# Where the first half's rows are turned at three layer ends, where a gate turn stands, and buffers of their own for the memory rows

## The reference

```python
def rms_norm(x, gain):
    y = x * lax.rsqrt(jnp.mean(x * x, axis=-1, keepdims=True) + RMS_EPS)
    return y * gain

for i in range(2):                                   # NSA, then SSD
    hn = rms_norm(h, gains[0])
    m = nsa_mixer(hn, ...) if i == 0 else ssd_mixer(hn, ...)
    h = h + rms_norm(m, gains[1])
    f = conv_ffn(rms_norm(h, gains[2]), ...)         # up, conv, silu * , down
    h = h + rms_norm(f, gains[3])
# second block, one layer
mem_n = rms_norm(mem, mem_norm)
u = rms_norm(h, norm_pre_mix)
y_mix, q_mem = gdn_branch(u @ gdn_w_in, ...)
mem_k, mem_v = jnp.split(mem_n @ w_mem_kv, 2, axis=-1)
y = jnp.concatenate([y_mix, memory_attention(q_mem, mem_k, mem_v)], axis=-1) @ w_out
h = h + rms_norm(y, norm_post_mix)
h = h + rms_norm(swiglu(rms_norm(h, norm_pre_ffn), ...), norm_post_ffn)

# inside the NSA mixer, 48 columns of the projection become the gates
gates = sigmoid(proj[..., kv_end:]).reshape(b, s, g, hpg, 3)
```

## Time and profile before

| | us |
|---|---|
| three runs | 1214.59, 1219.58, 1211.85; median 1214.59 |
| the profiled execution | 1215.68 |
| its span in the profile | 1213.9 |
| PE busy / DVE busy / ACT busy | 1180.3 / 847.2 / 651.3 |
| mean granted clock of PE, share of full | 0.998 |

### The profile page before, as it was taken

The page is one execution under the profiler, slowest core; times in us unless marked ns, Lnnn a source line. Parts: engine busy times, 40 slices in busy tenths (PEclk is TensorE's granted clock), DMA queues, the critical chain, the costliest instruction groups (busy, mean ns, idle before and its releaser), DMA issues.

```text
span 1213.9 us, 23231 instructions
## 1 busy us (share of the span) xinstructions
PE 1180.3 (97%) x9876; PEld 1079.3 (89%) x9876; DVE 847.2 (70%) x1299; ACT 651.3 (54%) x1171; POOL 149.0 (12%) x143
## 2 busy tenths in 40 slices
PE   8999999999999999999999999999999999999998
PEld 8887779999879898977999988899989877999986
DVE  6578867888557888886788875857577776655542
ACT  4557646666445666644666663565434534644431
POOL 1220000000002333100000000103443411000000
PEclk9999999999999999999999999999999999999999
DMA  8842135665634443353655664442232322755540
GB/s 304 266 140 88 62 103 218 209 204 183 238 106 148 177 182 141 113 175 112 243 187 197 208 242 156 176 174 105 94 118 71 111 100 87 279 181 198 182 169 35
DMA packets 31623, 196.68 MB, mean 162 GB/s; under 512 B 4000, under 2 KB 5664, under 8 KB 9376
## 3 DMA queue, kind: packets, MB, share of 16 engines
q1 hardware_dynamic: 27504, 185.17, 43.0%
q10 hardware_dynamic: 4016, 10.03, 2.6%
HBM read 193.09 MB, written 1.05 MB: 160 GB/s over the span
## 4 chain that ended last, share of the span: by engine, by line
PE 86%; DVE 6%; ACT 3%; issue 2%; POOL 1%; DMA 1%; ACTq 0%; DVEq 0%; POOLq 0%; SPq 0%
PE bank L514 24%; PE bank L516 23%; PE bank L515 23%; DVE wlo L502 2%; PE bank L1860 1%; ACT whi L495 1%; PE bank L1097 1%; PE bank L1154 1%; PE bank L1181 1%; DMA raw<-in_wall 1%; DVE xT L704 1%; PE bank L2506 1%; PE bank L688 1%; PE bank L2972 1%; PE bank L2449 1%
## 5 line engine op out<-in xcount | busy, mean ns | idle before, releaser
L502 DVE TENSOR_TENSOR wlo<-raw,whi 128x1024 fp32r<-128x1024 f32 (+1 forms) x325 | 390.0, 1237 | 92.8 <-ACT whi L495 92.1
L514 PE MATMUL bank<-xT,wlo 128*128 128x256 f32 x1544 | 434.4, 281 | 6.2 <-DVE xc L1566 2.1
L516 PE MATMUL bank<-xT,whi 128*128 128x256 f32 x1544 | 428.6, 278 | 0.0
L515 PE MATMUL bank<-xT,whi 128*128 128x256 f32 x1544 | 428.6, 278 | 0.0
L495 ACT ACTIVATE whi<-raw 128x1024 fp32r<-128x1024 f32 (+1 forms) x349 | 349.5, 1048 | 115.8 <-PE bank L516 82.8
L514 PEld LDWEIGHTS bank<-xT,wlo 128*128 128x128 f32 x1544 | 288.6, 187 | 10.6 <-issue 3.9
L515 PEld LDWEIGHTS bank<-xT,whi 128*128 128x128 f32 x1544 | 288.8, 187 | 0.9 <-issue 0.5
L516 PEld LDWEIGHTS bank<-xT,whi 128*128 128x128 f32 x1544 | 288.5, 187 | 0.2
L633 POOL TENSOR_TENSOR rr<-rr,nhalf 128x1 f32<-128x1 f32 x34 | 24.8, 729 | 714.4 <-DVE rr L621 526.7
L514 PE MATMUL bank<-whi,xT 128*128 128x256 f32 (+1 forms) x352 | 104.6, 297 | 6.6 <-DVE xT L704 6.6
L514 PE MATMUL bank<-whi,gT 128*128 128x512 f32 x264 | 104.4, 396 | 0.0
(11 more groups left out here) (369 smaller groups left out, 1654.1 us busy)
## 6 DMA issues: line engine op xcount, KB each, us to landing
raw<-in_wall SPq DMA_DIRECT2D x173, 1024.0 KB, 4.9
grow<-in_rows ACTq DMA_DIRECT2D x13, 512.0 KB, 5.6
h<-in_x SPq DMA_DIRECT2D x4, 256.0 KB, 5.6
dsk<-in_rows ACTq DMA_DIRECT2D x4, 256.0 KB, 3.5
memx<-in_mem ACTq DMA_DIRECT2D x1, 1024.0 KB, 9.9
out<-h SPq DMA_DIRECT2D x4, 256.0 KB, 2.1
masks<-in_masks SPq DMA_DIRECT2D x1, 580.0 KB, 12.6
D<-Tx ACTq DMA_DIRECT2D x4, 128.0 KB, 6.0
```

The lines of the kernel that those rows point to most:

```text
L502: e.tensor_tensor(wlo[i % NHL][:, o:o + w], raw[i % NRAW][:, o:o + w], whi[i % NHL][:, o:o + w], SUB).then_inc(*up("dve.low", p))
L514: e.matmul(out, a[1], b[0], start=start, stop=False)
L515: e.matmul(out, a[0], b[1], start=False, stop=False)
L516: return e.matmul(out, a[0], b[0], start=False, stop=stop)
```

## The change

It has three parts. The reordering on PE at a layer's end stands in `pe_down`, which may call a function between its two halves n=0 and n=1; the callers give `pe_norm_turn(e, k, 0)` for the last chunk of t=1.

```diff
-        def pe_down(e, t, i, src, ks, base, start, stop, k0=0):
+        def pe_down(e, t, i, src, ks, base, start, stop, between=None):
...
                 if stop and t and n == 0:
                     d.then_inc(*up("pe.early", i))
+                if between and n == 0:
+                    between()
...
-        def pe_boundary(e, k, a=None):
-            pe_norm_turn(e, k, 0)
-            if a is not None:
-
-                e.wait_ge(*at("dve.norm", "mp", a, 0, 0))
-                e.wait_ge(*at("act.norm", "add", a, 0, 1))
-                pe_fill_first(e, FFN_AT.index(k), k)
-                pe_busy(e, 0, 6)
+        def pe_boundary(e, k, a):
+
+
+            e.wait_ge(*at("dve.norm", "mp", a, 0, 0))
+            e.wait_ge(*at("act.norm", "add", a, 0, 1))
+            pe_fill_first(e, FFN_AT.index(k), k)
+            pe_busy(e, 0, 6)
             pe_norm_turn(e, k, 1)
...
         def pe_ssd_first(e):
 
-            pe_norm_turn(e, 2, 0)
...
-                pe_down(e, t, C_GO + c, ygT, ks, 2 * t, c == 0, c == 5)
+                pe_down(e, t, C_GO + c, ygT, ks, 2 * t, c == 0, c == 5,
+                        (lambda: pe_norm_turn(e, 6, 0)) if (t, c) == (1, 5) else None)
...
-            pe_ffn(e, 0, 1)
+            pe_ffn(e, 0, 1, None, lambda: pe_norm_turn(e, 2, 0))
...
-                pe_down(e, t, C_SO + c, ysT, (2 * c, 2 * c + 1), 2 * t, False, c == 7)
+                pe_down(e, t, C_SO + c, ysT, (2 * c, 2 * c + 1), 2 * t, False, c == 7,
+                        (lambda: pe_norm_turn(e, 3, 0)) if (t, c) == (1, 7) else None)
```

```diff
+        ffd = ExitStack()
+        sb([128, 2, 22, 256], st=ffd, name="below")
+        mT = [sb([128, 8, 256], f32r, ffd, "mT") for _ in range(2)]
+        ffd.close()
...
+        def rows_of(k):
+            return mT if k == 4 else xT
...
             for i in range(2):
-                run(pe_tm(e, C_M + 2 + i, 6 + i, 256))
+                run(pe_tm(e, C_M + 2 + i, 6 + i, 256, None, mT))
...
+            split.to(C_M + 3)
+            for t in range(2):
+                act_norm_high(e, 5, t)
             split.to(C_M + 3 + AHEAD)
-            e.wait_ge(*at("pe.proj", C_M + 3))
-            for n in range(2):
-                for t in range(2):
-                    act_norm_high(e, 5, t, (n,))
...
+            for t in range(2):
+                dve_norm_low(e, 5, t)
             for i in range(2):
                 split.to(C_M + 2 + i + AHEAD)
                 e.wait_ge(*at("pe.proj", C_M + 2 + i))
...
-            for n in range(2):
-                for t in range(2):
-                    dve_norm_low(e, 5, t, (n,))
```

```diff
-                q = pe_fm(e, QC[c4], QB[c4])
-                next(q)
+                run(pe_fm(e, QC[c4], QB[c4]))
                 if c4 == 0:
                     e.wait_ge(*at("act.nsa", "sigmoid"))
                     pe_few_turn(e, aP[0], 4, 48).then_inc(*up("pe.nsa", "gates"))
-                run(q)
...
                 split.to(5 + c4 + AHEAD)
+                act_q(e, c4)
                 if c4 == 0:
                     e.wait_ge(*at("pe.nsa", "gates"))
```

More of the change, by code:

```diff
@@ L386, in build @@
         pr = [sb([128, 512], st=ffm, name="pr") for _ in range(2)]
+        sb([128, 1024], st=ffm, name="rest")
         memx = sb([128, 2, 1024], st=ffm, name="memx")
         ffm.close()
+        ffd = ExitStack()
+        sb([128, 2, 22, 256], st=ffd, name="below")
+        mT = [sb([128, 8, 256], f32r, ffd, "mT") for _ in range(2)]
+        ffd.close()
         sst = ExitStack()
@@ L414, in build @@
         y1 = xs[:, 512:1024]
+        gk = ExitStack()
+        kmT = sb([128, 4, 256], st=gk, name="kmT")
+        vm = sb([128, 2, 512], st=gk, name="vm")
+        gk.close()
         gd = ExitStack()
@@ L429, in build @@
         ma = ExitStack()
-        kmT = sb([128, 4, 256], st=ma, name="kmT")
-        vm = sb([128, 2, 512], st=ma, name="vm")
         qmT = sb([128, 4, 256], st=ma, name="qmT")
@@ L519, in pe_ready, with pe_fm @@
             e.wait_ge(*at(low_on(i), ENDS[i] - 1))
-        def pe_fm(e, i, bank, layer=None):
+        def pe_fm(e, i, bank, layer=None, rows=xT):
             pe_ready(e, i)
@@ L530, in pe_fm @@
                     t = pe_three(e, banks[bank][:, 256 * m:256 * m + 256], [v[:, k, 128 * m:128 * m + 128] for v in w],
-                                 [x[:, k, :] for x in xT], k == 0, k == 7)
+                                 [x[:, k, :] for x in rows], k == 0, k == 7)
                 if m == 0:
@@ L534, in pe_fm, with pe_tm @@
             t.then_inc(*up("pe.proj", i))
-        def pe_tm(e, i, bank, n, layer=None):
+        def pe_tm(e, i, bank, n, layer=None, rows=xT):
             pe_ready(e, i)
@@ L543, in pe_tm @@
                 for k in range(8):
-                    t = pe_three(e, banks[bank][:, 256 * s:256 * s + n], [x[:, k, 128 * s:128 * s + 128] for x in xT],
+                    t = pe_three(e, banks[bank][:, 256 * s:256 * s + n], [x[:, k, 128 * s:128 * s + 128] for x in rows],
                                  [v[:, k, :] for v in w], k == 0, k == 7)
@@ L696, in act_norm_high @@
                 e.wait_ge(*at("pe.norm", k, t, n))
-                e.activation(xT[0][:, 4 * n:4 * n + 4, 128 * t:128 * t + 128], four(turn_bank(k, t, n)),
+                e.activation(rows_of(k)[0][:, 4 * n:4 * n + 4, 128 * t:128 * t + 128], four(turn_bank(k, t, n)),
                              ACTF.Copy).then_inc(*up("act.norm", "high", k, t, n))
@@ L701, in dve_norm_low @@
             for n in ns:
-                hi, lo = [x[:, 4 * n:4 * n + 4, 128 * t:128 * t + 128] for x in xT]
+                hi, lo = [x[:, 4 * n:4 * n + 4, 128 * t:128 * t + 128] for x in rows_of(k)]
                 e.wait_ge(*at("act.norm", "high", k, t, n))
@@ L747, in pe_busy @@
                 e.matmul(banks[bank][:, 0:350], identb[:, :], negb[:, 0:350], start=True, stop=True)
-        def pe_boundary(e, k, a=None):
-            pe_norm_turn(e, k, 0)
-            if a is not None:
-                e.wait_ge(*at("dve.norm", "mp", a, 0, 0))
-                e.wait_ge(*at("act.norm", "add", a, 0, 1))
-                pe_fill_first(e, FFN_AT.index(k), k)
-                pe_busy(e, 0, 6)
+        def pe_boundary(e, k, a):
[3 more added lines that the diff above has]
+            pe_busy(e, 0, 6)
             pe_norm_turn(e, k, 1)
-            if a is not None:
-                pe_busy(e, 0, 3)
+            pe_busy(e, 0, 3)
         F_UP = [at_mat[f"up{f}"] for f in range(3)]
@@ L827, in down_groups, with pe_ffn @@
             return [[c] for c in range(11 - HOLD)] + [list(range(11 - HOLD, 11))]
-        def pe_ffn(e, f, k, mid=None):
+        def pe_ffn(e, f, k, mid=None, early=None):
             c = F_UP[f]
@@ L851, in pe_ffn @@
                         e.wait_ge(*at("dve.ffn", "low", f, j))
-                        pe_down(e, t, c + j, gT, (2 * j, 2 * j + 1), 2 * t, j == 0, j == 10)
+                        pe_down(e, t, c + j, gT, (2 * j, 2 * j + 1), 2 * t, j == 0, j == 10,
+                                early if t and j == 10 else None)
         def act_tap(e, f, j, s, dst):
@@ L1013, in act_nsa_in @@
                                      "p t (h b) -> p t b h", b=3), ACTF.Copy).then_inc(*up("act.nsa", "gates"))
-                act_q(e, c4)
         def act_q(e, c4):
@@ L2171, in pe_gdn_in @@
             for i in range(2):
-                run(pe_fm(e, C_M + i, 4 + i))
+                run(pe_fm(e, C_M + i, 4 + i, None, mT))
             for t in range(2):
@@ L2972, in tensor @@
                 e.matmul(banks[0][:, 0:128], ident, ident, start=True, stop=True)
-            pe_boundary(e, 0)
+            for t in range(2):
+                pe_norm_turn(e, 0, t)
             for _ in range(8):
```

## The result

| | before | changed |
|---|---|---|
| median of 15 runs, us | 1214.83 | 1207.20 |
| range of the runs, us | 1211.85 to 1219.58 | 1205.87 to 1211.67 |
| profiled execution, its own time | 1215.68 | 1207.32 |
| its span | 1213.9 | 1205.5 |

The ratio is 0.9932, with a 95% interval of 0.9919 to 0.9945: by the ratio 8.3 us less, between 6.7 and 9.8; the two medians of the table differ by 7.6. A second comparison, on another chip, gave 0.9934 (0.9909 to 0.9959). The forecast was 1205.1 within 1201.5 to 1210.5, and no difference over 1%.

The account below looks back on a forecast made before the run. PE was taken as the bound, busy 1180.3 of 1213.9 us, leaving waits and clock. Gains 4.0 + 2.2 + 3.3 = 9.5 off 1215.68 give 1206.2; with the median 1.1 lower, 1205.1, range 1201.5 to 1210.5.

Parts of the forecast that it names:

- Layer ends: At k=2, 3 and 6, turning inside the last chunk starts later work earlier: 1.4, 1.3 and 1.3, sum 4.0 us.
- the forecast's 0.4: At a layer's end, the wait for the low parts shrinks from 1.66 us to 0.4.
- the margin: At layer ends, the first half of `xs` is ready 0.33 us before the turn wants it, 0.25 at k=6.
- The terms of 1.3 at k=3 and k=6: The wait behind the second turn hangs on DVE's chain, which comes 1.3 us earlier, so 1.3 instead of 1.4.
- GDN's entry: With own buffers for the turned rows, the 2.10 us wait goes and a matmul step is 0.1 shorter: 2.2 us.
- cost for the move: At GDN's entry, the new buffer addresses were taken to cost nothing, since no row showed a cost.
- Gates: At the NSA gates, the wait for the sigmoid (1.61 us) and the slow clock behind it (1.66) go: 3.3 us.
- The clock falls anyway: Rival at the gates: the clock still falls, this part gives 1.6, sum 7.8, time 1206.8 us; chance 0.12.
- The turn waits in the chunk: Rival at layer ends: `xs` is late, with 1.4 us each they give nothing, sum 5.5, time 1209.1; chance 0.06.
- The weights do not follow: Rival at the gates: weights come no earlier or time is handed back, sum 6.2, time 1208.4 us; chance 0.07.
- The clock falls at the turns: Rival at the three layer ends: PE drops to 1.2 GHz; with 12 us each, 1223 us; chance of slower 0.03.
- More than the waits: Rival: ACT and DVE chains with short waits (second turns, scan) shrink too, over 12.1 us, about 1201; chance 0.08.

Follow-up runs that it names:

- ends_only: The kernel before with only the reordering at the three layer ends (k=2, 3, 6); ratio 0.9964, 4.4 us less.
- turn_early: The changed kernel with the first half's turn ahead of both halves of the last chunk at the three layer ends; ratio to the kernel before 0.9945.
- change_again: The changed kernel itself, unaltered, run once more on another chip; ratio to the kernel before 0.9934, span 1205.8 us.
- gates_fill: The kernel before, order unchanged, with 12 dummy 256-column matmuls in front of PE's wait for the sigmoid; ratio 1.0003.
- mem_only: The kernel before with only the memory's own buffers and the earlier copies of the k=5 rows; ratio 1.0002.
- no_gates: The changed kernel with the NSA gates' turn put back into the middle of chunk 5; ratio to the kernel before 0.9962.
- gates_later: The changed kernel with six spare copies on ScalarE in front of the sigmoid, delaying it; ratio to the kernel before 0.9963.

## Why the prediction was right

**Layer ends: 4.0 forecast, 4.0 measured** (1.39, 1.23 and 1.38 in the trace; 1.4, 1.2 and 1.4 in `ends_only`). The wait left is 0.27 by the shown end of the last output matmul, or 0.44 from where its 0.23 us are over, so the forecast's 0.4 came; `xs` started 0.87 us ahead of its turn, where a start 0.54 ahead is enough, so the margin was 0.33, as read. `turn_early` shows the price on the other side of it. The terms of 1.3 at k=3 and k=6 came near for another reason than the one argued. PE starts the new layer 1.4 earlier at all three, 4.2 in sum; the 4.0 takes k=3 at its second half. There 1.23 is left because the products up to the second turn ran at the step of 0.118 there and at 0.113 before: from the first product to the turn it is 5.69 us against 5.54. `xs` was no limit, it started 0.76 ahead of that turn. In `change_again` this stretch has 0.113, and 1.36 is left. What DVE's chain takes is 0.06: where PE is quick, the wait behind the second turn is 0.59 instead of 0.53, as at k=6.

**GDN's entry: 2.2 forecast, 1.78 measured** at the gate columns, 1.58 behind them. The wait went in full. What was mis-sized is the work around it: the 96 `vm` products ran at 0.113 us each before and at 0.119 now, which gives 95 x 0.005 = 0.5 back. This is no accident of one execution: the step is 0.113 in all five profiles without the memory's buffers and 0.119 in all nine with them. The 48 products behind the gate columns take 5.73 us instead of 5.54, another 0.19. I had taken no cost for the move, since no row showed one: that term, put at nothing, is where the sum was wrong.

The traces say more on its cause. The copies that now run beside the `vm` products end at 769.0 on ACT and at 772.9 on DVE, but PE stays slow to the last product. Here are 6 us behind them, in the changed kernel and at about the same products in the kernel before:

```profile
773.00:779.00 6.00, 6.00 (x53) 6.00 (x52) 5.06 (x5) 2.01 (x2) 0.00 (x0) 1.00 0.87 343
```

```profile
778.00:784.00 6.00, 6.00 (x56) 6.00 (x55) 3.57 (x4) 2.01 (x2) 0.00 (x0) 1.00 0.99 419
```

And the 96 `kmT` products ahead of the turn, where no copy has moved, take 11.52 us in all nine profiles with `mT`, 11.19 in the kernel before and 11.39 or 11.40 in the four others without. So the slower step comes with the buffer that PE reads, and the moved copies don't explain it. What about the buffer does it, its place for instance, was not tried. The sum missed a gain, too: half clock follows the wait of 2.10 us in three of the five kernels that have it and in none of nine that do not. The one profile of before was one of the two without.

**Gates: 3.3 forecast, 3.0 measured** (55.82 to 52.85). The wait gives 1.52 and not 1.61: the turn stood 1.73 behind the product in front of it (42.35 to 44.08) and stands 0.21 behind it now (45.26 to 45.47). The rest is the clock, 1.53 by `gates_fill` where 1.66 was forecast. Over all profiles the mask product stands between 52.25 and 53.14 in seven kernels with this part and at 55.78, 55.82, 56.03 and 58.36 in four without: 3.2 us between the means if the last is left out. Its wait was 1.45, 1.72, 2.16 and 2.83 in the four, so the profile that the forecast rested on showed the smallest. Half clock comes with the wait in all five profiles with 1.40 us or more at this place, and in none of the nine with 0.58 or less. By the rule of the Trainium skill (TensorE: Matmul & The Clock Gate, HAM oscillation) each of these waits is too short to cost the clock; the traces contradict it. It need not come in every execution: of 130 timed runs of these kernels seven had a mean clock of 1.000, so no slow stretch at all (three of 83 of the kernel before, one each of `mem_only` and `no_gates`, two of `gates_later`). How long PE waited in those is not on record.

**From the parts to the time.** The trace adds up: 3.17 (at the first turn behind NSA, 167.54 to 164.37) + 1.39 + 1.23 + 1.78 + 1.38 = 8.95. Between the places 0.7 is lost, of which the `kmT` products are 0.33 and those behind the gate columns 0.19; the last end gains 0.1 more by its second half, where it was the kernel before that ran at 0.118. That makes the 8.4 of the spans, and the forecast was 9.5. The second error is in the reference point. I set the median 1.1 us below the profiled execution, because it was so for three runs of before. In the changed kernel the profiled execution (1207.32) is nearly the median (1207.20). The two errors, 1.1 and 1.0, make up the 2.1 between 1205.1 and 1207.2. Some luck was in it: both profiles had all three FFNs at the step of 0.113 and no half clock at GDN's entry, so none of what differs by several us from one execution to the next fell between them.

**The rivals.** *The clock falls anyway* (the first of the list, called the second in the text on the gates): no. `gates_fill` has the same order, no long wait and no fall; `gates_later` has the wait again, and the fall. *The turn waits in the chunk:* no wait at any of the three. *The weights do not follow:* chunk 6 and the scores came 3 us earlier. *The clock falls at the turns:* no fall at a layer end in any of the 14 profiles, neither with the turn inside the chunk nor, in five profiles and fifteen places, with the old wait of 1.66 us behind it. *More than the waits:* the whole stayed under 12.1 us. What there was beyond the waits was not in short waits, as I had it, but in half clock behind GDN's entry, for which the profile of before gave no sign.

## What to carry to other kernels

A transpose that waits for a vector chain can be set inside the last matmuls of the step before. It gains as much as there is PE work behind it, as long as its input is ready; work out that margin from both sides, since past it the gain is lost again (`turn_early`: 0.69 of 1.4 at the first half, 1.02 with the second). A wait of PE's is priced too low by its length, if half clock can follow it: look at several executions, because one shows only one draw. Data in a new buffer can cost what the old one did not, even where no instruction is added. And when single executions differ by 4 us for reasons of their own, a change of 2 us is judged by the start of the first instruction behind it, in several traces, not by a dozen times.

## What was not expected of the hardware

- **Two steps at full clock.** Back-to-back 256-column matmuls with granted clock 1.00 start 0.113 or 0.118 us apart, with no value between for hundreds of matmuls. In the FFNs it changes only where transposes interrupt, and which it will be differs between profiles of like kernels. Its cause stays open. The products that read `mT` have a third, 0.119 to 0.120.
- **Half clock follows some waits, not others of like length.** In the profiles: gates, waits of 1.40 to 2.83 us: five of five. GDN's entry, 2.10: three of five. Near 400 us, about 1.9, for `xc` of the state-space layer: five of fourteen. Layer ends, 1.66 behind eight transposes: none of fifteen. The slow stretch was 3.4 us long each time but one, the 6.8 us that began inside the wait of 2.83.
- **A slow stretch need not cost.** Near 400 us PE loses 1.4 to 1.5 us to it, and by 430 all but 0 to 0.3 is back, since PE waits for DVE in the state-space scan anyway. At GDN's entry nothing comes back, and it costs 1.7.
